# Nine gate/up column blocks by seven products and two plain, instead of eight and three

## The reference

```python
h = rms_norm(x, g_mix)
... # attention and state-space branches, merged into mix
x = x + mix @ w_out
h2 = rms_norm(x, g_ffn)
x = x + (silu(h2 @ w_ffn_gate) * (h2 @ w_ffn_up)) @ w_ffn_down   # D_FF = 2816
```

## Time and profile before

| | |
|---|---|
| median of 3 runs | 869.68 us (869.61 to 870.47) |
| the profiled execution | 867.67 us |
| its span, from the first to the last instruction | 865.9 us |
| TensorE busy | 856.4 us, 99% |
| VectorE busy | 568.0 us, 66% |
| granted TensorE clock | 1.000 |

### The profile page before, as it was taken

One profiled execution on the slowest core, in us unless ns is written; L12 is line 12 of the kernel. 1 busy time (PEld: TensorE's weight loads), 2 busy tenths in 40 slices (PEclk: granted clock), 3 DMA queues, 4 the chain that ended last, 5 costly groups with the idle time before them and its releaser, 6 DMA issues.

```text
span 865.9 us, 15093 instructions
## 1 busy us (share of the span) xinstructions
PE 856.4 (99%) x5203; PEld 733.5 (85%) x5203; DVE 568.0 (66%) x753; ACT 366.0 (42%) x575; POOL 259.2 (30%) x271
## 2 busy tenths in 40 slices
PE   9999999999999999999999999998999999999998
PEld 8788788888887878877887888888999999888886
DVE  5558976577924444534488565889999999533334
ACT  6312343323245656756434443344555455222221
POOL 3789996010020000001220220046666664000000
PEclk9999999999999999999999999999999999999999
DMA  8439236634365442413545333323333333222222
GB/s 308 146 101 234 79 122 140 221 129 141 118 220 174 149 152 84 147 48 96 146 135 188 98 97 98 98 74 98 103 114 112 108 97 121 76 97 96 96 73 98
DMA packets 103495, 108.89 MB, mean 126 GB/s; under 512 B 11712, under 2 KB 69296, under 8 KB 103328
## 3 DMA queue, kind: packets, MB, share of 16 engines
q1 hardware_dynamic: 96544, 94.25, 34.6%
q10 hardware_dynamic: 5504, 10.52, 3.7%
q0 software_dynamic: 1408, 3.61, 1.9%
HBM read 94.38 MB, written 13.96 MB: 125 GB/s over the span
## 4 chain that ended last, share of the span: by engine, by line
PE 49%; DVE 3%; POOL 1%; issue 1%; ACT 0%; DMA 0%; SPq 0%; ACTq 0%; DVEq 0%; POOLq 0%
PE ps L1848 18%; PE ps L1868 13%; PE ps L1535 12%; PE ps L1810 6%; DVE late L1517 1%; DVE w_lo L1407 1%; DVE h_lo L1403 0%; DVE wx_t L1407 0%; DVE late L1331 0%; DVE w_lo L664 0%; DVE hT_lo L1337 0%; DVE late L1370 0%; DVE late L1377 0%; DMA w_raw<-in_w_ffn_up 0%; POOL late L634 0%
## 5 line engine op out<-in xcount | busy, mean ns | idle before, releaser
L664 DVE TENSOR_TENSOR w_lo<-w_raw,w_hi 128x1024 fp32r<-128x1024 f32 x109 | 140.0, 1284 | 207.8 <-ACT w_hi L658 207.6
L658 ACT ACTIVATE w_hi<-w_raw 128x1024 fp32r<-128x1024 f32 x109 | 115.3, 1058 | 279.0 <-PE ps L1535 162.7
L1535 PE MATMUL ps<-w_hi,hT_hi 128*128 128x512 f32 x280 | 109.7, 392 | 1.6 <-DVE w_lo L664 0.9
L1535 PE MATMUL ps<-w_hi,hT_lo 128*128 128x512 f32 x280 | 109.0, 389 | 0.0
L1535 PE MATMUL ps<-w_lo,hT_hi 128*128 128x512 f32 x280 | 109.0, 389 | 0.0
L496 POOL TENSOR_TENSOR early<-early 128x16 f32<-128x16 f32 (+6 forms) x129 | 91.4, 708 | 23.1 <-ACT early L681 13.1
L1535 PE MATMUL ps<-hT_hi,w_hi 128*128 128x512 f32 x224 | 91.5, 408 | 0.0
L1535 PE MATMUL ps<-hT_hi,w_lo 128*128 128x512 f32 x224 | 87.7, 392 | 0.0
L1535 PE MATMUL ps<-hT_lo,w_hi 128*128 128x512 f32 x224 | 87.4, 390 | 0.0
L1848 PE MATMUL ps<-hT_hi,wx_t 128*128 128x256 f32 x384 | 72.1, 284 | 2.3 <-DVE wx_t L1407 2.3
L1848 PE MATMUL ps<-h_hi,w_hi 128*128 128x256 f32 x256 | 72.5, 283 | 0.3 <-DVE w_lo L1407 0.3
(11 more groups left out here) (247 smaller groups left out, 1803.4 us busy)
## 6 DMA issues: line engine op xcount, KB each, us to landing
w_raw<-in_w_in SPq DMA_DIRECT2D x108, 256.0 KB, 3.4
w_raw<-in_w_ffn_down SPq DMA_DIRECT2D x44, 256.0 KB, 2.7
w_raw<-in_w_ffn_gate SPq DMA_DIRECT2D x64, 128.0 KB, 2.2
w_raw<-in_w_ffn_up SPq DMA_DIRECT2D x64, 128.0 KB, 2.3
z_d<-early ACTq DMA_DIRECT2D x7, 1024.0 KB, 4.9
late<-z_d SPq DMA_DIRECT2D x96, 64.0 KB
w_raw<-in_w_out SPq DMA_DIRECT2D x16, 256.0 KB, 2.9
late<-z_d SPq DMA_DIRECT2D x12, 256.0 KB
```

The source lines that it names most:

```text
L658: nc.scalar.activation(w_hi[:, j % WSPL], w_raw[:, j % WRAW], ACT.Copy).then_inc(w_hi_done, 1)
L664: nc.vector.tensor_tensor(w_lo[:, j % WSPL], w_raw[:, j % WRAW], w_hi[:, j % WSPL].bitcast(F32), ALU.subtract).then_inc(w_lo_done, 1)
L1535: ins = T.matmul(ps[:, bank0 + m], lhsT, rhs, start=first and h == 0 and k == 0, stop=last and h == 1 and k == 2)
```

## The change

FP becomes 2, so blocks 0 and 1 are plain and 2 to 10 go by seven products. All preparation of partners and of the first operands, which was laid around the steps of plain blocks 1 and 2, is laid around those of block 1: on VectorE partner 0 now comes before the last plain load's `lo`, operands 0 to 2 come before difference 3 and the evacuation of the last plain block, and partners and operands 3 to 6 alternate behind it. The gating of the last plain block (`gated`) moves from before half 1 of the first seven-product block to behind its operand i = 3. ScalarE's list follows the same order. TensorE's loop over the plain blocks is written out.

```diff
-FP = 3
+FP = 2
...
             silus(0, 2)
-            for j in range(1, 5):
+            for j in range(1, 4):
                 hi(W_FFN + j + 4, j)
-                if j >= 3:
-                    partner_hi(j - 3)
+                if j > 1:
+                    partner_hi(j - 2)
+            for i in range(2):
+                op_hi(FP, 0, i, True)
+            for i in range(2, 7):
+                partner_hi(i)
+                op_hi(FP, 0, i, True)
             for m in range(2):
-                act.wait_ge(ffn_evac, 4 + m + 1)
-                nc.scalar.activation(sg[:, m], sg[:, m], ACT.Silu).then_inc(silu_done, 1)
-            for j in range(1, 4):
-                hi(W_FFN + j + 8, j)
-                if j < 3:
-                    partner_hi(j + 1)
-            for i in range(3):
-                op_hi(FP, 0, i, True)
-            partner_hi(4)
-            for i in (3, 4):
-                op_hi(FP, 0, i, True)
-            partner_hi(5)
-            op_hi(FP, 0, 5, True)
-            partner_hi(6)
-            op_hi(FP, 0, 6, True)
-            for m in range(2):
-                act.wait_ge(ffn_evac, 8 + m + 1)
+                act.wait_ge(ffn_evac, 4 * FP - 4 + m + 1)
                 nc.scalar.activation(sg[:, m], sg[:, m], ACT.Silu).then_inc(silu_done, 1)
...
                 for i in range(7):
                     op_lo(f, 1, i)
-                    if i == 3 and not first:
+                    if i == 3 and first:
+                        gated(f - 1)
+                    elif i == 3:
                         gated_up(f - 1)
...
             lo(W_FFN + 6, 2)
-            for n in range(3):
+            for n in range(2):
                 difference(n)
+            partner_lo(0)
             lo(W_FFN + 7, 3)
+            partner_lo(1)
+            difference(2)
+            for i in range(2):
+                op_lo(FP, 0, i)
+            partner_lo(2)
+            op_lo(FP, 0, 2)
             difference(3)
-            partner_lo(0)
-            lo(W_FFN + 8, 4)
-            partner_lo(1)
-            swiglu(1)
-            for j in range(1, 4):
-                lo(W_FFN + j + 8, j)
-                if j < 3:
-                    partner_lo(j + 1)
-            for i in range(3):
+            columns_out(FP - 1)
+            for i in range(3, 7):
+                partner_lo(i)
                 op_lo(FP, 0, i)
-            partner_lo(4)
-            columns_out(FP - 1)
-            for i in (3, 4):
-                op_lo(FP, 0, i)
-            partner_lo(5)
-            op_lo(FP, 0, 5)
-            partner_lo(6)
-            op_lo(FP, 0, 6)
-            gated(FP - 1)
             half_a(FP, True)
             half_b(FP)
...
-            with pe.Fori(1, FP) as f:
+            for f in range(1, FP):
                 for j in range(4):
                     ffn(f, j)
```

More of the change, by code:

```diff
@@ L1800, in ffn @@
                     if j == 0:
-                        if isinstance(f, int):
+                        if f == 0:
                             pe.wait_ge(dve_evac, DE_MIX + m + 1)
@@ L1804, in ffn @@
                             pe.wait_ge(ffn_evac, 4 * f - 3 + m)
-                    if isinstance(f, int) and m == 0:
+                    if f == 0 and m == 0:
                         pe.wait_ge(h2_lo_done, 2 * j + 2)
```

## The result

The changed kernel takes 873.44 us (median of 6 runs, 872.60 to 876.12); the kernel before takes 869.79 us in the 6 runs beside it. The ratio is 1.0048, with a 95% interval of 1.0036 to 1.0059: slower by 0.5%, or by some 4 us. The forecast was 873.7 us. The profiled execution of the changed kernel took 872.68 us, with a span of 870.8 us.

A forecast was written before the change was run, and what follows sets the result against it. TensorE, busy 99%, bounds the kernel, except where VectorE prepares the first seven-product block. TensorE's -1.60 us plus standing of 9.0 against 3.36 us gives +4.0 us on the median 869.68: 873.7 us, range 870.4 to 877.5.

The forecast's parts named there:

- TensorE's term: Gate/up stage: one plain block of 21.76 us becomes a seven-product block of 20.16 us, -1.60 us, clock at full speed.
- The total: Whole kernel: -1.60 us on TensorE plus standing of 9.0 against 3.36 us gives +4.0 us, 873.7 us.
- The four sums of half 0: Under plain block 1: GpSimd's sums start at 548.1 us, each costing VectorE 1.10 us; TensorE waits 3.4 us before product 3.
- The sums of half 1: First seven-product block: sums lengthen VectorE's operand 5, partner 6 and operand 6; TensorE waits 1.4 and 2.5 us.
- The statement that ScalarE keeps ahead: Preparation of the first seven-product block: ScalarE's roundings are ready before VectorE needs them, or wait for VectorE itself.
- The lead in the later blocks: Later seven-product blocks: VectorE's smallest lead of 2.8 us shrinks by 1.5 to 1.3 us; nothing beyond 20.16 us each.
- rival (b): Second or third seven-product block: the lead does not suffice, +1 to +3.5 us on top, 875 to 877.5 us; chance 0.17.
- Rival (c): Under block 1: the first four sums miss SBUF work, leaving 4.6 us of standing, 869.3 us, no change; chance 0.11.
- Rival (d): First seven-product block: VectorE and GpSimd do not exclude each other, standing 0, -5.0 us, 864.7 us; chance 0.06.

The follow-up runs named there:

- made narrow: Changed kernel, GpSimd's four sums for half 0 of the first seven-product block cover 8 columns instead of 512, the rest constant: 869.68 us, ratio 1.0009.
- all eight sums narrow: Changed kernel, GpSimd's eight sums for both halves of the first seven-product block cover 8 columns instead of 512, the rest constant: 864.53 us, ratio 0.9951.
- its two best edits: Each alone on the changed kernel: first two sums of half 1 released by operand three instead of five, 870.05 us; gating back before half 1, 871.94 us.
- the kernel with FP = 3: Kernel before, gating moved behind operand 3 of half 1 and first two sums of half 1 released by the third operand: 865.34 us, ratio 0.9953.
- the sums released early: Changed kernel, first two sums of half 1 released by the third operand of half 0 instead of the fifth; the third waits for the fifth: 870.05 us.
- the kernel with the late release: Changed kernel, sums of half 1 released by the seventh operand of half 0 instead of the fifth: 873.87 us, ratio 1.0048.
- the four experiments of the 869.36 us: Half 0's sums narrow (869.68 us), half 1's sums early on the changed kernel (870.05), both edits on the kernel before (865.34), late release (873.87).

## Why the prediction was right, and where it was not

*TensorE's term, -1.60 us.* Right: 20.16 us for the second seven-product block after, 21.76 for a plain one in the earlier trace rows. The profiled spans differ by 870.8 - 865.9 = 4.9 us: 29.44 - 23.52 = 5.92 for the first block, less 1.60, and 0.56 because the block began at 556.93 instead of 556.37 us. That 0.56 is in the stages ahead, where the two do not differ; in the other profiles with two plain blocks this start lies anywhere from 556.5 to 560.0 us. The term also held the clock at full speed. That is so in both profiles, but of the six runs of the changed kernel only one had a mean granted clock of 1.000, one had 0.998 and four 0.996.

*The total.* The forecast added 4.0 us. The block and TensorE's term give 5.92 - 1.60 = 4.3 us, the two profiled executions differ by 5.0 us, the medians by 3.65. So the agreement of the medians with the forecast to 0.3 us is closer than the forecast's own terms are good for, and in part luck.

*The four sums of half 0.* Right in place (first sum at 548.80, forecast 548.1) and in price (2.24, 2.23, 1.70, 1.70 us, and 4.36 us when they were made narrow). Product 3 started at 564.48 us; forecast was 564.13, and with the later start 564.7.

*The sums of half 1.* Here a step failed. The prediction had operand 5, partner 6 and operand 6 of half 0 each lengthened by a sum (568.6, 570.8, 572.5 us) and TensorE standing 1.4 and 2.5 us before products 5 and 6. None of them was lengthened: operand 6 began at 568.96 us, and TensorE stood 0.2 us before each product. GpSimd, kept out, delivered later instead, so VectorE waited for ScalarE and ScalarE for GpSimd, and TensorE stood 1.92 us before product 1 of half 1, which the forecast had at nothing. The gating met two sums instead of one, and the wait behind it was 2.43 us and not 1.4. In sum 9.28 us against 9.0: half 0 had 4.2 us of standing where 7.6 were forecast, half 1 had 5.1 where 1.4 were. The total came out although its parts did not; that GpSimd's work must be done at some time makes this plausible, but the close agreement is luck. The statement that ScalarE keeps ahead was wrong for operands 1 and 2 of half 1, where VectorE waited for it 3.28 and 0.21 us, and it for GpSimd.

*The lead in the later blocks.* Right: no standing after 581.95 us, so rival (b) did not occur. What spoke for (b), that VectorE had no idle time in the earlier trace rows, was misread: the row at 563.16 us in the earlier trace rows shows 2.43 us of it. *Rival (c)*: with four sums out of the way the standing was 4.92 us and the time that of before, as (c) had it (4.6 us, 869.3); its condition did not occur by itself. *Rival (d)*: with all eight sums narrow the time was 864.53 us, where (d) had 864.7 for sums that cost nothing. But (d) had no standing and the kernel had 1.37 us of it; by (d)'s own sum that would be 866.1 us. So the match is in part luck, and its condition was false. The experiment takes away the length of the sums along with the exclusion of the two engines, and does not part the two.

So the change is slower because it gives VectorE one plain block less (21.8 us) in which to do its preparation, at a place where GpSimd's sums take 4.4 us from it; the gain of 1.6 us on TensorE is worth less than the 5.9 us that TensorE stands longer. That FP = 2 could be made to win was not shown. With its two best edits apart it reached 870.05 and 871.94 us, and the standing of 3.2 to 3.3 us before product 3 is in both; the two together were not run; the kernel with FP = 3 had none left at 865.34 us.

## What to carry to other kernels

When work leaves the bound engine, ask first which other engine was working under its cover. Here 21.8 us of cover were given up for 1.6 us, and TensorE was standing 3.4 us there already. Take the price of a short instruction from rows in which its neighbour runs as well as from rows in which it is alone (1.70 against 0.60 us), and lay GpSimd's work beside VectorE's reads of PSUM: one number in a wait, one added wait and one moved gating gave 0.5% (4.0 us, 3.3 of them in the block), twice what the larger rearrangement could have gained on TensorE. A part of a change can be good for one order and bad for another, as the gating's move was (-2.3 us and +1.5 us), so it is tried by itself.

## What was not expected of the hardware

**GpSimd can be kept out for several instructions of VectorE in a row.** In the changed kernel from 566.24 to 570.1 us, and so in every kernel with its order and the release at five operands: the same sum took 5.15 us in two more of them, 6.36 us with the gating in its old place, where six instructions of VectorE passed it, and 4.06 us even when it had only 8 columns. SBUF — State Buffer, section "Who interferes with whom", of the Trainium skill, says that of the two engines the one that issues first has the ports that they share for its whole instruction, and the other blocks; this agrees with each single step, but does not say who comes next, and here VectorE came next four times running. With the sums released early, the third sum, there from 569.45 us during the same partner step, got in at the next change of instruction, and so did the first sum of half 1 in the kernel before, there from 580.49 us (2.21 us long). What decides it stays open.

**A long standing can cost more than itself.** In some executions TensorE's granted clock falls after it. In the profile of the kernel with the late release it did twice. A row has the stretch and its length, the busy time and the instructions of PE, PEld, DVE, ACT and POOL, then granted clock, DMA share and GB/s:

```profile
561.10:564.40 3.30, 0.27 (x3) 0.06 (x1) 3.30 (x6) 3.30 (x6) 0.00 (x0) 1.00 0.00 0
564.45:568.70 4.25, 4.25 (x23) 4.25 (x24) 4.25 (x5) 3.39 (x6) 0.00 (x0) 0.60 0.00 0
568.70:573.10 4.40, 4.40 (x38) 4.40 (x38) 1.51 (x3) 0.28 (x1) 3.34 (x3) 1.00 0.42 119
573.10:579.40 6.30, 5.11 (x39) 4.50 (x37) 5.70 (x4) 4.32 (x9) 6.22 (x5) 1.00 0.31 87
579.40:581.90 2.50, 0.27 (x3) 0.06 (x1) 2.50 (x4) 1.46 (x3) 1.33 (x1) 1.00 0.00 0
581.94:585.70 3.76, 3.76 (x19) 3.76 (x20) 3.76 (x6) 0.67 (x2) 1.58 (x1) 0.55 0.42 119
```

After a standing of 3.2 and one of 2.4 us the clock was at its lower level, 1.2 of 2.4 GHz, for most of the next 4 us, and matmuls came 0.21 us apart instead of 0.12. The block took 30.94 us instead of 29.44, though all of VectorE's steps were as in the changed kernel. Only the second fall cost time: product 1 of half 1 started 17.67 us into the block here and 17.66 us in the changed kernel, since VectorE was late for it anyway, and the 1.5 us came behind it. Behind the standing before product 3 the clock fell in three more of the profiles, to a mean of 0.56 to 0.61 over 3.3 to 3.9 us. The changed kernel's own profile, with the same gaps, shows 1.00 throughout. The kernel before, whose largest gap is 2.5 us, has a mean clock of 1.000 in 9 of the 23 runs beside the four experiments of the 869.36 us, with a median of 868.2 us, and of 0.998 in the other 14, with a median of 869.5 us. The kernel before with the gating moved, and the one with the sums early as well, have no gap over 1.4 us, and 1.000 in all of their 9 and 6 runs; the kernel with the eight narrow sums has none either, and 1.000 in three of its 5 runs, 0.999 in two. So moving the gating gained 1.2 us against the runs of the kernel before at 1.000 (868.2 to 866.97 us), which is what its block says (1.1 us), and the clock may account for the other 1 us of the 2.3 us. That is an inference: the kept profile of the kernel before is at 1.000, so where the clock falls in the others is not shown.
